# Moving filler matmuls ahead of a chain of small matmuls in a recurrent decoder step

## The reference

```python
h = _rmsnorm(x, norm_mix)
u = h @ w_in                        # columns for three branches and three gates
o_a = _rwkv7(u_a, ...)              # 8 heads x 64: S = S*w + sa (x) (kk*a) + v (x) k ; o = S r
o_b = _retention(q, k, v, ...)      # 4 heads x 128, rotary q and k, chunked
o_c = _hgrn2(q, log f, k, v, ...)   # 4 heads x 128, chunked
x = x + (sum(sigmoid(gate_i) * (o_i @ w_branch_i)) @ w_out)
x = x + (silu(h2 @ w_gate) * (h2 @ w_up)) @ w_ffn_out     # h2 = _rmsnorm(x)
```

## Time and profile before

| | us |
|---|---|
| median of three runs (lowest, highest) | 2747.41 (2746.34, 2748.84) |
| the profiled execution | 2749.1 |
| its span, first to last instruction | 2747.4 |
| TensorE (PE) matmuls busy | 2619.6 |
| GpSimd (POOL) busy | 1368.4 |
| VectorE (DVE) busy | 1283.0 |
| ScalarE (ACT) busy | 685.2 |

### The profile page before, as it was taken

The page is one execution under the profiler, slowest core; times in us unless marked ns, Lnnn a source line. Parts: engine busy times, 40 slices in busy tenths (PEclk is TensorE's granted clock), DMA queues, the critical chain, the costliest instruction groups (busy, mean ns, idle before and its releaser), DMA issues.

```text
span 2747.4 us, 66281 instructions
## 1 busy us (share of the span) xinstructions
PE 2619.6 (95%) x25812; PEld 2485.5 (90%) x25812; DVE 1283.0 (47%) x1830; ACT 685.2 (25%) x1196; POOL 1368.4 (50%) x1179
## 2 busy tenths in 40 slices
PE   5999999999999999999979999999999999999996
PEld 4989889899899999999978898998998999999996
DVE  4535535345246633336455353452463556333454
ACT  3322323223224211112132142231332322110122
POOL 4425446255255655556653461552553466555564
PEclk9999999999999999999989999999999999999998
DMA  4213122122126322212321221221221453222122
GB/s 172 66 41 103 55 68 95 34 88 76 37 92 210 116 85 84 91 58 81 100 89 51 76 90 33 88 78 37 93 66 54 145 164 100 92 84 87 59 84 81
DMA packets 84542, 233.61 MB, mean 85 GB/s; under 512 B 12176, under 2 KB 16288, under 8 KB 83312
## 3 DMA queue, kind: packets, MB, share of 16 engines
q1 hardware_dynamic: 66672, 188.40, 21.6%
q10 hardware_dynamic: 14112, 29.63, 2.8%
q0 software_dynamic: 3552, 12.56, 1.4%
HBM read 198.57 MB, written 31.98 MB: 84 GB/s over the span
## 4 chain that ended last, share of the span: by engine, by line
PE 79%; DVE 9%; PEld 4%; issue 3%; ACT 2%; DMA 2%; POOL 1%; SPq 0%; DVEq 0%; PEldq 0%; ACTq 0%; POOLq 0%
PE psP L643 43%; PE psQ L643 14%; PE psQ L707 10%; PEld psP L643 3%; PE psQ L700 3%; PE psQ L982 2%; PEld psQ L643 1%; PE psQ L955 1%; PE psP L972 1%; PE psP L707 1%; DMA W<-in_w_br 1%; PE psQ L947 1%; PE psP L966 1%; DVE BIG L1561 1%; DVE BIG L1510 1%
## 5 line engine op out<-in xcount | busy, mean ns | idle before, releaser
L501 POOL TENSOR_SCALAR WS<-W 128x512 fp32r<-128x512 f32 (+1 forms) x392 | 293.8, 749 | 842.9 <-PEq L637 446.9
L643 PE MATMUL psP<-HH,WS 128*128 128x272 f32 x2496 | 552.5, 307 | 28.1 <-DVE HL L1484 19.7
L643 PE MATMUL psP<-HH,WR 128*128 128x272 f32 x2240 | 470.0, 292 | 0.0
L643 PE MATMUL psP<-HL,WS 128*128 128x272 f32 x2240 | 469.9, 292 | 0.0
L643 PE MATMUL psP<-BIGR,WS 128*128 128x272 f32 x2976 | 425.4, 292 | 21.1 <-POOL WS L503 10.9
L643 PEld LDWEIGHTS psP<-HH,WS 128*128 128x128 f32 x2496 | 395.1, 192 | 51.7 <-issue 29.8
L643 PEld LDWEIGHTS psP<-BIGR,WS 128*128 128x128 f32 x2976 | 393.7, 190 | 29.8 <-issue 15.9
L503 POOL TENSOR_TENSOR WR<-W,WS 128x512 fp32r<-128x512 f32 x280 | 391.4, 1398 | 23.4
L643 PE MATMUL psQ<-BIGR 128*128 128x272 f32 x2848 | 388.7, 288 | 0.0
L643 PEld LDWEIGHTS psQ<-BIGR 128*128 128x128 f32 x2848 | 369.5, 188 | 0.2
L643 PEld LDWEIGHTS psP<-HL,WS 128*128 128x128 f32 x2240 | 359.3, 192 | 0.0
(11 more groups left out here) (281 smaller groups left out, 3276.2 us busy)
## 6 DMA issues: line engine op xcount, KB each, us to landing
W<-in_w_stage SPq DMA_DIRECT2D x88, 512.0 KB, 3.7
W<-in_w_f SPq DMA_DIRECT2D x88, 512.0 KB, 3.7
W<-in_w_gate SPq DMA_DIRECT2D x48, 512.0 KB, 3.9
W<-in_w_f SPq DMA_DIRECT2D x88, 256.0 KB, 2.6
gates_waiting<-GB ACTq DMA_DIRECT2D x48, 272.0 KB, 4.3
BIG<-gates_waiting SPq DMA_DIRECT2D x48, 272.0 KB, 3.0
W<-in_w_br SPq DMA_DIRECT2D x48, 256.0 KB, 2.7
W<-in_w_out SPq DMA_DIRECT2D x16, 512.0 KB, 3.7
```

The lines of the kernel that those rows point to most:

```text
L501: pool.tensor_scalar(high, src, 1.0, 0.0, ALU.mult, ALU.add).then_inc(high_part[q], 1)
L643: mm = pe.matmul(out[:, a, 0:HT], a_, x_[:, a * HT:(a + 1) * HT], start=(first and n == 0), stop=(last and n == 2))
```

## The change

The calls of `fill` in four places are moved. No instruction is added or removed; the list of filler steps and their order stay.

- In each merging step there were two runs, one ahead of the first job and one between the `square` and the second job: steps 12, 13 and 14, 15 in the first merging step, and step 16 and step 17 in the second. Now each has one run, ahead of its first job: 12, 13, 14 and 15, 16, 17.
- Ahead of the chunk chain there was one step, 19, and in each of the chain's first four chunks one, 20 to 23, between the start of S and the wait for U. Now all five stand ahead of the chain, and its first four chunks have none, as chunk 4 had none before. Chunks 5 to 7 keep their runs of three, three and two steps behind the output.

```diff
-                    for step, off, cur, prev, f0, f1, f2 in ((1, LO32, 1, "I4", 12, 14, 16), (3, LO64, 0, "M2", 16, 17, 18)):
+                    for step, off, cur, prev, f0, f1 in ((1, LO32, 1, "I4", 12, 15), (3, LO64, 0, "M2", 15, 18)):
                         fill(f0, f1)
                         for g in GR:
                             after(f"{prev}{g}")
...
                             square(l, ph, turn, "B_ropek", K["swap"][:], UB[:, TOK:2 * TOK])
-                        fill(f1, f2)
                         for g in GR:
                             after(f"M{step}{g}")
...
-                    fill(19, 20)
+                    fill(19, 24)
                     ob = job("A_out")
...
                         heads(b[:, 0, 0:HD], TK[:, 2, c], TK[:, 3, c], True, False)
                         if c:
                             heads(b[:, 0, 0:HD], K["eye64"], ST[c % 2], False, False)
-                        fill(*((20 + c, 21 + c) if c < 4 else (0, 0)))
                         after(f"U{c}")
```

## The result

The changed kernel took 2755.47 us, the median of 20 runs (2743.28 to 2763.88); 20 runs of the kernel before beside them took 2746.27 us (2735.18 to 2755.32). The ratio is 1.0032 (95% interval 1.0019 to 1.0045): slower by about 9 us, clear of noise; the interval reaches down to 0.19%. The profiled execution took 2758.7 us around a span of 2757.0.

A forecast was written before the change was run, and what follows sets the result against it. TensorE, busy 95% of the span, bounds the kernel. Losses of 0.31, 0.32 and 0.30 us a stage, 7.4 us in eight, took the profiled 2749.1 us to 2756.5; forecast median 2755 us, range 2747 to 2763.

The forecast's parts named there:

- The price of a step and of a run: Filler runs on TensorE: a step takes 0.754 us, a run of one 0.94, entering and leaving 0.19.
- The stalls at M2 and M4: Merging steps: TensorE stands still about 0.8 us for the sine product before group 1; losses 0.31 and 0.32 us a stage.
- The chain: Chunks 0 to 3 without filler: 2.72 us less inside, 3.02 us more in front, a loss of 0.30 us a stage.
- The sum: Both merging steps and the chunk chain together: 0.93 us lost a stage, 7.4 us in eight stages.
- The clock: Half-clock stretches inside the stages, none in merging steps or chain: two more or fewer, 3 us either way.
- Rival 2: Chunk chain: the clock falls, one half-clock stretch a stage, another 12 us, 2767 us; chance 0.07.
- Rivals 1, 3 and 4: 1: no M2/M4 stalls, 2745 us, 0.14; 3: half-clock stretches vanish, 2741 us, 0.03; 4: runs wait for weights, 2768 us, 0.03.

The follow-up runs named there:

- e3: Kernel before with each merging step's filler run in front and the square issued ahead of it, chain unmoved: 2738.36 us against 2740.60, ratio 0.9991.
- e6: The changed kernel timed once more beside the kernel before: 2753.31 us against 2741.60, ratio 1.0042.
- p3: Kernel before with the matmuls of I4 issued twice, three times for chunk 0, no filler step moved: 2754.36 us against 2744.93, ratio 1.0037.
- e2: Kernel before with only the chunk chain changed, merging steps as before: 2748.24 us against 2740.60, ratio 1.0024.
- b1: Kernel before with merging fills behind the square, output terms without U ahead of its wait, steps 20 to 23 behind the output: 2736.25 us, ratio 0.9963.

## Why the prediction was right, and where not

- **The price of a step and of a run** held: 3.96 us for five steps is 0.94 + 4 x 0.754.
- **The stalls at M2 and M4** are there, behind the sine product, at the place that the square's result leaves; e3 takes them away with the order of the PSUM places. Their size was off: TensorE went on 2.09 us after the square, as worked out (2.08), but the wait in the list is 0.41 us, not 0.5 to 0.8 (0.52 counted from starts as the 0.8 was), because M2 of group 0 began 1.11 us after the square and not 0.82; and groups 1 and 2 then took 0.73 us together, not 0.46 + 0.38, because the second follows the first without a gap. The later start of group 0 costs nothing, as group 1 waits anyway; the shorter groups are why a merging step lost 0.21 us, not 0.31.
- **The chain** lost 0.27 us (0.30 predicted). What I called late next, the copy of U, is what is waited for: 63 times, 0.19 us. A term that the prediction lacked is the late U of chunk 5 in the fourth stage: 1.1 us in the first profile, 2.8 us in two stages of e6.
- **The sum** was 5.6 us, not 7.4, and 5.7 us at equal clock in e6.
- **The clock** is the step that did not hold. I had put it at 3 us either way, as if the count of half-clock stretches were the same on average for both kernels. In e6 it isn't: the mean clock of the change is 0.0024 lower (standard error 0.0007), 6.4 us, all one way. In the first series, where the clock of before is on record for one run alone, 9.2 - 5.6 = 3.6 us are left for it and for the late U. p3 shows that a stage longer by the same 0.7 us loses about as much with every filler step in its place. The forecast met the median in part by luck: this made up for a sum that I had taken 1.8 us too high.
- **Rival 2** (half clock in the bare chain) holds for one stage of eight in the first profile and two in e6, none in e2: a small part of the loss, and a stall stood beside it each time. The Trainium skill's sentence on short idle times between groups ("TensorE: Matmul & The Clock Gate", A second HAM failure mode: psum-queue depth-cycling), as the prediction applied it, would have had the clock fall in every chain; 9.62 us at 1.00 disagree. Rivals 1, 3 and 4 are out: the stalls are in the trace, the stretches did not go away, and no run waited for weights.

## What to carry to other kernels

Work that covers a wait belongs where the wait ends last, and a wait on a buffer place counts as much as one on data: here one short product between two jobs held the place that the second job needed. In a loop of latencies between engines, covering one wait only hands it to the next; the gain comes where both are covered, each by other work. A list of waits leaves out a gap that the modelled ends of the matmuls cover; the distance between starts shows it. And where half-clock stretches come and go between runs of one kernel, as here, a change of a few microseconds should be timed beside a control that has the same length and moves nothing, with the granted clock written down for every run.

## What was not expected of the hardware

Adding 0.34, 0.58 and 0.69 us to each of eight stages cost 9 us, nothing that shows, and 9 us. The time of one and the same kernel spread over 21 us (2732.07 to 2753.21 for the 23 runs of before beside p3 and b1), and a straight line in the mean granted clock of a run (0.982 to 0.989) accounts for 89% of the variance. TensorE also stood still a few times for 0.2 to 1.5 us with no engine, queue or semaphore behind it in the trace, the longest each time at one place, ahead of U of chunk 5 in the fourth stage of a layer; what these stalls are was not tried.
